# A bidirectional mLSTM in chunks of 128 tokens with a carried state, and three experts asked for in routing, in a two-layer float32 kernel

## What is computed

```python
b = jnp.cumsum(lf, axis=-1)
d_log = jnp.where(tril, b[..., :, None] - b[..., None, :] + ig[..., None, :], -jnp.inf)
inter = b + m_st[..., None]
m_t = jnp.maximum(inter, jnp.max(d_log, axis=-1))
s = jnp.einsum('bhtd,bhsd->bhts', q, k) * jnp.exp(d_log - m_t[..., None])
w_inter = jnp.exp(inter - m_t)
num = einsum(s, v) + w_inter[..., None] * einsum(c_st, q)
den = jnp.sum(s, axis=-1) + w_inter * einsum(n_st, q)
h = num / jnp.maximum(jnp.abs(den), jnp.exp(-m_t))[..., None]
c_new = decay * c_st + einsum(ws, v, k);  n_new = decay * n_st + einsum(ws, k)
...
h_m = rmsnorm(h_fwd + h_bwd, g_mlstm) * sigmoid(o)
```

## Time and profile before

| | |
|---|---|
| median of the timed runs | 3332.91 us (3331.67, 3332.91, 3337.18) |
| the profiled execution | 3332.51 us |
| its span, first to last instruction | 3330.8 us |
| PE busy, of the span | 2955.4 us (89%) |
| DVE, ACT, POOL busy | 1328.8, 585.3, 345.6 us (40%, 18%, 10%) |
| granted TensorE clock, mean | 0.949 |
| moved by DMA | 356.83 MB, mean 107 GB/s |

### The profile page before, as it was taken

How to read it: one execution, slowest core, us unless ns; L and a number is a source line. 1 busy time by engine, 2 the same in 40 slices (tenths; PEclk the granted TensorE clock), 3 DMA queues, 4 the chain that set the end, 5 groups by cost and what they waited for, 6 DMA issues and landing times. The chain is left out here.

```text
span 3330.8 us, 42568 instructions
## 1 busy us (share of the span) xinstructions
PE 2955.4 (89%) x17472; PEld 2247.0 (67%) x17472; DVE 1328.8 (40%) x2355; ACT 585.3 (18%) x1386; POOL 345.6 (10%) x511
## 2 busy tenths in 40 slices
PE   5988788999999999999999899888996949888883
PEld 4855566567777788888888788677875845455551
DVE  4645555822224442434343564453525351111114
ACT  2213213810000210100000241332002011111111
POOL 1011131000000100000000100452002011111112
PEclk9989899999999999999999999898998969999997
DMA  3100012011112111111112431001110259999995
GB/s 123 51 13 1 1 38 82 30 53 38 50 48 98 37 47 57 38 51 51 51 41 62 90 50 27 2 2 37 51 32 9 109 211 381 416 413 408 405 369 214
DMA packets 127058, 356.83 MB, mean 107 GB/s; under 512 B 14089, under 2 KB 58377, under 8 KB 109457
## 3 DMA queue, kind: packets, MB, share of 16 engines
q1 hardware_dynamic: 114464, 336.09, 28.0%
q0 software_dynamic: 10512, 16.80, 1.3%
q10 hardware_dynamic: 1888, 1.22, 0.1%
HBM read 343.18 MB, written 31.46 MB: 112 GB/s over the span
## 5 line engine op out<-in xcount | busy, mean ns | idle before, releaser
L427 PE MATMUL banks<-hT_upper,split_weights 128*128 128x512 f32 x2304 | 746.4, 401 | 15.1 <-PEq L193 8.6
L427 PEld LDWEIGHTS banks<-hT_upper,split_weights 128*128 128x128 f32 x2304 | 435.9, 189 | 117.0 <-issue 22.1
L418 PE MATMUL banks<-split_weights,hT_upper 128*128 128x512 f32 x1536 | 485.4, 398 | 22.5 <-DVE hT_lower L136 9.0
L427 PE MATMUL banks<-hT_lower,split_weights 128*128 128x512 f32 x1152 | 451.4, 392 | 0.0
L418 PEld LDWEIGHTS banks<-split_weights,hT_upper 128*128 128x128 f32 x1536 | 292.4, 192 | 85.8 <-issue 18.7
L418 PE MATMUL banks<-split_weights,uT_upper 128*128 128x512 f32 x1024 | 315.9, 390 | 0.0
L418 PE MATMUL banks<-split_weights,hT_lower 128*128 128x512 f32 x768 | 304.5, 396 | 0.0
L2784 PE MATMUL banks<-expert,ex_xT 128*64 128x256 f32 (+1 forms) x1632 | 263.5, 399 | 45.7 <-DMA expert<-in_w_up 21.2
L427 PEld LDWEIGHTS banks<-hT_lower,split_weights 128*128 128x128 f32 x1152 | 218.2, 189 | 54.9 <-issue 11.2
L2784 PEld LDWEIGHTS banks<-expert,ex_xT 128*64 128x64 f32 (+1 forms) x1632 | 171.4, 150 | 101.4 <-issue 60.1
L418 PEld LDWEIGHTS banks<-split_weights,uT_upper 128*128 128x128 f32 x1024 | 192.1, 188 | 39.5
(11 more groups left out here) (452 smaller groups left out, 3810.7 us busy)
## 6 DMA issues: line engine op xcount, KB each, us to landing
expert<-in_w_gate SPq DMA_DIRECT2D x51, 1024.0 KB, 13.3
expert<-in_w_up SPq DMA_DIRECT2D x51, 1024.0 KB, 22.2
expert<-in_w_down SPq DMA_DIRECT2D x51, 1024.0 KB, 24.9
raw_weights<-in_w_in SPq DMA_DIRECT2D x38, 1024.0 KB, 5.5
raw_weights<-in_w_up SPq DMA_DIRECT2D x16, 1024.0 KB, 5.3
raw_weights<-in_w_down SPq DMA_DIRECT2D x16, 1024.0 KB, 5.0
hT<-in_w_gate SPq DMA_DIRECT2D x13, 1024.0 KB, 11.6
hT<-in_w_up SPq DMA_DIRECT2D x13, 1024.0 KB, 23.4
```

Source lines behind the costliest of these rows:

```text
L418: last = pe.matmul(bank, acts[x][:, r * KT // 2 + k, m * P:(m + 1) * P].bitcast(F32R), w[y][:, k, :].bitcast(F32R), start=(r == 0 and k == ...
L427: last = pe.matmul(out, w[x][:, k, c0:c0 + P].bitcast(F32R), acts[y][:, k, t0:t0 + nt].bitcast(F32R), start=(k == 0 and x == y), stop=(k = ...
```

## The change

`mlstm_inputs` gets two more rows and a small one: with `m_end` the maximum at a chunk's last token (in the direction's order) and `m_ref` that of the chunk before, `W` = m_ref - M (the state's weight at each token), `WS` = A - m_end (a key's weight in the state), and `dec_row` = m_ref - m_end (the state's own decay, 8x8). `T1`, `W`, `WS` and `dec_row` are exponentiated by ACT at i == 15.

`mlstm` is written anew. Its 16 units (N = 2 x TT) are one chunk of 128 tokens in one direction, for all four heads; directions alternate, forwards from chunk 0 and backwards from chunk 7 (`unit`). Units 0 to 7 (n < DONE) meet a chunk for the first time, units 8 to 15 for the second, when the sum over both directions can be normalized and gated. A unit's weights are one 128x512 tile; banks: 0 for the maxima, 1 for the decays, 2 and 3 for the scores, 4 to 7 in two pairs for numerators, denominators and state updates. The weights, weighted keys and maxima of unit n + 2 and the scores of n + 1 are asked for ahead of unit n's products. The old `Pt` of [P, (TT * (TT + 1) + KT) * P] becomes `work` of [P, KT * S + 2 * S].

In the diff, `x` in engine rows is the memory that holds queries and keys, `ml_work` is `work`.

```diff
-def mlstm_inputs(c, hT, whole, qk_raw, qkT, v_sb, og, row):
+def mlstm_inputs(c, hT, whole, qk_raw, qkT, v_sb, og, row, dec_row):
...
-                    nc.scalar.activation(row(T1), row(T1), ACT.Exp)
+                    for r in (T1, W, WS):
+                        nc.scalar.activation(row(r), row(r), ACT.Exp)
+                    nc.scalar.activation(dec_row, dec_row, ACT.Exp)
...
+            s_dve.done(nc.vector.tensor_tensor(by_chunk(W), along(m_ref), by_chunk(M), ALU.subtract))
+            s_dve.done(nc.vector.tensor_tensor(by_chunk(WS), by_chunk(A), along(m_end), ALU.subtract))
+            s_dve.settle(dve)
+            nc.vector.tensor_tensor(dec_row, m_ref[:, :], m_end[:, :], ALU.subtract).then_inc(m_ready, 1)
...
+            def m_rows(n):
+                d, j = unit(n)
+                if n:
+                    pe.wait_ge(exp_done, n)
+                for h in range(M_HEADS):
+                    last = nc.tensor.matmul(c.bank(0)[:, h * P:(h + 1) * P], c.k["pick8"][:, 4 * d + h, :], row(M)[:, chunk(j)],
+                                            start=True, stop=True)
+                last.then_inc(mrow_there, 1)
...
+            def scores(n):
+                d, j = unit(n)
+                if n:
+                    pe.wait_ge(weighted, n)
+                for i in range(2):
+                    for h, b, rows_of in heads_of(i):
+                        last = nc.tensor.matmul(SCORES[:, b, i * P:(i + 1) * P], qkT[rows_of, 2 + i, chunk(j)],
+                                                qkT[rows_of, i, chunk(j)], start=True, stop=True)
+                last.then_inc(scores_there, 1)
...
+            for n in range(N):
+                d, j = unit(n)
+                if n + 2 < N:
+                    m_rows(n + 2)
+                if 2 <= n + 1 < N:
+                    decays(n + 1)
+                if n + 1 < N:
+                    scores(n + 1)
...
+                elif n < DONE + 2:
+                    pe.wait_ge(first_taken, n - 1)
+                else:
+                    pe.wait_ge(second_taken, n - 1 - DONE)
+                if n < N - 2:
+                    pe.wait_ge(kw_ready, n + 1)
+                    for i in range(2):
+                        for h, b, half_rows in heads_of(i):
+                            nc.tensor.matmul(c.psum[half_rows, out_bank(n) + i, 2 * V1:3 * V1], k_weighted[:, n % 4, h, :],
+                                             v_sb[:, j, h, :], start=True, stop=True)
...
+                pe.wait_ge(weighted, n + 1)
+                for i in range(2):
+                    for h, b, rows_of in heads_of(i):
+                        if n >= 2:
+                            nc.tensor.matmul(c.bank(out_bank(n) + b)[:, i * V1:(i + 1) * V1], q_scaled[rows_of, n % 2, i, :],
+                                             state[rows_of, d, i, :], start=True, stop=False)
+                    for h, b, _ in heads_of(i):
+                        last = nc.tensor.matmul(c.bank(out_bank(n) + b)[:, i * V1:(i + 1) * V1], weights[:, n % 4, place(h), :],
+                                                v_sb[:, j, h, :], start=(n < 2), stop=True)
+                last.then_inc(out_there, 1)
...
+        @block.scalar
+            for n in range(N):
...
+                if n + 2 < N:
+                    exps(n + 2)
+                if n < DONE:
+                    act.wait_ge(r_ready, n + 1)
+                    for h in range(M_HEADS):
+                        last = nc.scalar.activation(h_of(t, h), num(n, h), ACT.Copy, scale=r_den[:, n % 2, place(h):place(h) + 1])
+                    last.then_inc(first_taken, 1)
+                else:
+                    act.wait_ge(second_taken, n - DONE + 1)
+                    for h in range(M_HEADS):
+                        s_act.settle(act)
+                        last = nc.scalar.activation(junk[:, :], h_of(t, h), ACT.Square, accum_out=ss[:, t, h:h + 1])
...
+        @block.vector
+            for n in range(N):
+                if n + 1 < N:
+                    weigh(n + 1)
+                    if n + 1 >= 2:
+                        scale_q(n + 1)
+                if n < N - 2:
+                    update(n)
+                finish(n)
+                if n - 1 >= DONE:
+                    gate(n - 1)
...
+EARLY = 3
...
-            for i in range(SLOTS - 1):
+            for i in range(EARLY):
                 expert = experts.number(sp, slice(i, i + 1))
...
-            gate_up(SLOTS - 1)
-            down(SLOTS - 1)
+            sp.wait_ge(idx_ready, 2)
+            for i in range(EARLY, SLOTS):
+                gate_up(i)
+                down(i)
```

More of the change, by code:

```diff
@@ L1 @@
+import math
 from contextlib import ExitStack
@@ L624, in copy_out, with unit, chunk @@
[L624 to L627, removed]
-        block = mem.enter_context(nc.Block())
+        block = mem.enter_context(nc.Block())
+        I, X, T1, DCUM, A, M, W, WS = range(8)
+        def unit(n):
+            return n % 2, n // 2 if n % 2 == 0 else TT - 1 - n // 2
+        def chunk(j):
+            return slice(j * P, (j + 1) * P)
@@ new lines, in heads_of, with out_bank, num, h_of @@
+        def heads_of(i):
+            return [(2 * i + b, b, slice(b * M_QK, (b + 1) * M_QK)) for b in range(2)]
+        def out_bank(n):
+            return 4 + 2 * (n % 2)
+        def num(n, h):
+            return c.bank(out_bank(n) + h % 2)[:, h // 2 * V1:h // 2 * V1 + M_V]
+        def h_of(t, h):
+            return hs[:, t // 2, t % 2, h * M_V:(h + 1) * M_V]
+        def place(h):
+            return 2 * (h % 2) + h // 2
+        SCORES = c.psum[:, 2:4, 0:HALF]
+        K_PAIRS = [(j, TT - 1 - j) for j in range(TT // 2)]
@@ new lines, in _ @@
+            for which, r in ((0, A), (1, T1), (2, WS)):
+                for m in range(TT):
+                    nc.tensor.transpose(c.bank(4)[:, which * 64 + m * 8:which * 64 + m * 8 + 8], row(r)[:, chunk(m)], c.k["ident"][0:8, 0:8])
+            for d in range(2):
+                for i in range(2):
+                    for h, b, half_rows in heads_of(i):
+                        last = nc.tensor.matmul(c.psum[half_rows, 5, (2 * d + i) * TT:(2 * d + i + 1) * TT], c.k["pick8"][:, 4 * d + h, 0:M_QK],
+                                                dec_row, start=True, stop=True)
@@ new lines, in update @@
+            def update(n):
+                d, j = unit(n)
+                dve.wait_ge(out_there, n + 1)
+                for i in range(2):
+                    new = c.bank(out_bank(n) + i)[:, 2 * V1:3 * V1]
+                    old = state[:, d, i, :]
+                    if n < 2:
+                        last = nc.vector.tensor_copy(old, new)
+                    else:
+                        last = nc.vector.scalar_tensor_tensor(old, old, dec[:, d, i, j:j + 1], new, ALU.mult, ALU.add)
+                    if i == 0:
+                        s_dve.done(last)
+                s_dve.settle(dve)
+                last.then_inc(state_ready, 1)
@@ new lines, in gate @@
+            def gate(m):
+                t = unit(m)[1]
+                dve.wait_ge(rstd_ready, m - DONE + 1)
+                for h in range(M_HEADS):
+                    last = nc.vector.scalar_tensor_tensor(h_of(t, h), h_of(t, h), rstd[:, t, h:h + 1], og[:, t, h * M_V:(h + 1) * M_V],
+                                                          ALU.mult, ALU.mult)
+                last.then_inc(gated, 1)
+            copy_k(0)
+            weigh(0)
+            for p in range(1, 4):
+                copy_k(p)
@@ new lines, in _ @@
+            for n in range(N):
+                if n + 1 < N:
[7 more added lines that the diff above has]
+                    gate(n - 1)
+            gate(N - 1)
+            for m in range(DONE + 1, N, 2):
+                dve.wait_ge(hT_there, m - DONE + 1)
+                nc.vector.tensor_copy(qkT[:, :, chunk(unit(m)[1])], c.bank(m - DONE).rearrange("p (a n) -> p a n", a=4))
```

354 lines of the change are left out of this document (181 added, 173 removed).

## The result

| | before | after |
|---|---|---|
| median of the timed runs | 3332.29 us (3330.45 to 3337.18, 4 runs) | 3250.97 us (3245.43 to 3263.79, 4 runs) |
| profiled execution, its span | 3332.51, 3330.8 us | 3255.43, 3253.6 us |
| mLSTM block | 207.4 us | 138.7 us |
| expert stage, SP's first issue to the end | 618.6 us | 616.8 us |

After over before is 0.9759, 95% interval 0.9726 to 0.9792: **81 us faster**, where 102 were forecast (3230.5 us). The changed kernel's times spread over 18 us, those of the kernel before over 7.

A forecast was written before the change was run, and what follows sets the result against it. It took the mLSTM block as bound by engines' work and handovers, the expert stage by DMA bytes. Block 207.4 to 109 us (98.5) plus experts 3.5 gave 102 off 3332.5: 3230.5 us, range 3213 to 3274.

The forecast's parts named there:

- ahead of the loop, with the cold start: mLSTM block's start: transposes, decay factors, first row maxima, table load and exponentials, 11 us, plus 4 for cold start.
- 16 units, handovers, clock drops: mLSTM loop: 16 units less what first and last leave out, 77.4 us, plus 3 for handovers and 4 for drops.
- expert edit, gain: Expert stage: three experts asked for early instead of four, first gather lands 5 us earlier; net gain 3.5 us.
- 8 us for the clock: mLSTM block: allowance for half clock, 4 us for the cold start and 4 for drops as in the delta rule.
- Rival 1: mLSTM block stays at half clock, every unit PE-bound at 9.2 us, block 163 us, kernel 3285 us; chance 0.20.
- mixture: mLSTM block between full clock and the half clock of rival 1, kernel around 3255 us; chance 0.07.
- the case that the forecast stood on: mLSTM block at full clock, kernel 3215 to 3246 us; chance 0.58.
- rival 2: mLSTM unit costs what a retention chunk does, 6.9 us bound by its own chain; block 129, kernel 3251 us; chance 0.11.
- ACT's chain: mLSTM second half: row maxima wait for ACT's exponentials, which stand behind its squares; 5.4 us a unit.
- the 3 us for handovers: mLSTM block: handovers not counted elsewhere, as PE's last product must land, a few tenths a unit; 3 us.
- the prediction's own estimate of a drain: mLSTM units: 0.27 us per change of tile form instead of 0.15, 1 us more a unit, 16 us in all.
- Rival 3: mLSTM block: no overlap between units, 12.75 us each, block 224 us, kernel 13 us slower at 3346 us; chance 0.01.

The follow-up runs named there:

- full_rows: The change, with the products of row maxima and decays reading 128 rows, 120 of them zeros, instead of 8: 3216.7 us, ratio 0.9652.
- hot_start: full_rows with 13 more dense products, read by nobody, on PE at the end of mlstm_inputs: 3213.6 us, ratio 0.9649.
- warm: full_rows for units 0 to 5, with 8-row products of row maxima and decays from unit 6 on: 3251.0 us, ratio 0.9749.
- maxima_full: The change, with 128 rows only in the products of the row maxima, the decays left at 8: 3214.3 us, ratio 0.9653.
- the two fillers: The change with two more unread 256-column products per unit from the third on: of 128 rows 3230.6 us, of 8 rows 3285.4 us.

## Why the prediction was right in kind and wrong in size

| term | forecast | measured, the change | measured, full_rows |
|---|---|---|---|
| ahead of the loop, with the cold start | 15 | 13.3 | 12.7 |
| 16 units, handovers, clock drops | 84.4 | 116.7 | 73.3 |
| behind the last products | 9 | 8.7 | 8.7 |
| mLSTM block, sum | 108.4 | 138.7 | 94.7 |
| expert edit, gain | 3.5 | 4.1 (means of stages) | |

Without its 8 us for the clock the forecast is 100.4, which full_rows' 94.7 answer to. The loop is counted from the row maxima of unit 2, at 220.1 us, to the end of the last values' products, at 336.8 (220.2 and 293.5 in full_rows), so that 43 of the 44 us between the two blocks lie in it:

```profile
336.07 0.71 PE L773 MATMUL banks<-v_m,ml_work 128*128 128x129 f32 x4
```

**The term that failed is the clock.** The prediction took "4 us for the cold start and 4 for drops as in the delta rule (0.96 over some 80 us)". Measured, the change's block is 44 us longer than the one of full_rows, which differs from it by rows of zeros and, for a few us, by one change of tile form a unit; and 2.4 of full_rows' 94.7 are cold start (hot_start). The step that went wrong is the choice of the row: of the earlier trace rows the window at 251 to 254, PE busy throughout and 0.50 granted right behind 4 us of nothing but 8-row products, was the nearest to this block, and the delta rule, with 0.96, has no such products in it. I set against it that "scores to values are 3.4 us of dense work in each unit", and took it for granted that work by which PE is busy is work that holds the clock. It did not: 0.50 at 18.00 of 18.00 us busy.

**Rival 1 is what happened,** for most of the block. It said 9.2 us a unit where 9.04 were measured, from a price of 4.9 where a unit with eight changes of form takes 5.03 at full clock, and a ratio of 1.87 where 9.04 / 5.03 is 1.80: two small errors that nearly cancel. The block had a mean clock of 0.60 and not 0.50, since there were full-clock stretches near 230 and 245, and for the most part from 322 us on. So the time fell where the prediction had its mixture, "around 3255", with a chance of 0.07. That was too little: clock states that change within the block were a case of their own, next to "always up" and "always down", and they are what the prediction's own windows of other stages (0.96) show. The time lies inside the stated range of 3213 to 3274, but not by the case that the forecast stood on (full clock, 3215 to 3246). It is also the 3251 of rival 2, by luck: units there cost 6.9 us with PE idle, and here 9.04 with PE busy.

**At full clock the working holds.** PE's unit was priced at 4.9 us and is 5.03 with the eight changes of form that were priced (warm) and 4.85 with seven (full_rows): 0.99, 0.59, 0.64 and 0.59 for maxima, decays, scores and update, and 2.04 for the two rounds. For the second half 5.4 us a unit were worked out from ACT's chain. In full_rows the row maxima of unit 12 begin at 266.61 and those of unit 14 at 276.98, two units apart, 5.2 us each, and in front of both PE waits for ACT as the prediction said. These are the only two such waits: the earlier units of the second half still take 4.85.

```profile
266.61 1.16 PE L707 MATMUL banks<-ml_m_row,c_pick_wide 128*128 128x128 f32 x8 [0.41 <-ACT ml_work L814]
271.56 1.06 PE L707 MATMUL banks<-ml_m_row,c_pick_wide 128*128 128x128 f32 x8
276.98 1.16 PE L707 MATMUL banks<-ml_m_row,c_pick_wide 128*128 128x128 f32 x8 [0.40 <-ACT ml_work L814]
```

In the change itself this loop is hidden, since 9.04 is more than 5.2. In full_rows the loop of 73.3 us has no room for the 3 us for handovers: PE is busy for 18.00 of 18 us in the first half, and the forecast's 5.4 for all eight units of the second was too much.

**The change of tile form** was put at 0.15 us, and the prediction's own estimate of a drain, 0.27, would have added 16 us. (The Trainium skill, TensorEngine Tiling (Array Packing), "Key Properties", says that a change of tiling mode drains TensorE, and gives no time for it.) At 288.01 in full_rows the state products follow the scores in the same form, without a change between them. Elsewhere there is one on either side: the scores take 0.64 us to the next row (233.69 to 234.33) and the state products 0.43 (234.92 to 235.35). Here it is 0.55 and 0.32:

```profile
287.46 0.71 PE L728 MATMUL banks<-x 64*128 64x128 f32 x8
288.01 0.39 PE L791 MATMUL banks<-ml_work 64*128 64x129 f32 x4
288.33 0.71 PE L794 MATMUL banks<-v_m,ml_work 128*128 128x129 f32 x4
```

So a change costs about 0.09 us in the row ahead of it and 0.10 in the row behind, 0.19 together, and the 0.18 between 5.03 and 4.85 says the same. The trace agrees with the skill that a change has a price; its size lies nearer to the 0.15 of the sum than to 0.27. Eight of them are 1.5 us of a unit.

**Small terms.** The masking of 128x512 was taken at 1.05 us and took 0.64, a plain value between the bounds of 0.29 and 1.2; nothing hung on it. The row work in mlstm_inputs was costed at nothing, with DVE's 4.03 us of idle time as its cover, and cost 0.16. Rival 2 (6.9 us a unit from retention's own chain) is out: with the clock up, PE never idles in the first half. Rival 3 is out by the overlap that the trace shows.

**Experts.** The mechanism was right: the first use 5 us earlier was 4.5, and a short hole took the place of the first and of most of the second. The rule weighed against it (the Trainium skill, DMA: Bandwidth & Descriptors, "Queues, rings and completion order": queues share an engine packet by packet) was taken to give 0. The trace disagrees with that conclusion for this gather, 9.4 us behind four experts and 4.7 or 5.3 behind three, though the gathers of the stage still land after 9.0 in the median; whether the turns themselves are as the skill has them, no run here shows.

## What to carry to other kernels

Price a stretch of small products twice, at 1.00 and at 0.50, and decide between them by a row of the same rows and columns, not by how busy PE is. Where PE is the bound and its clock low, try to pad the contraction to 128 rows with zeros. It costs no product and no column, but memory and the time to write the zeros (here on an idle engine): in this kernel it gave another 34 us, two fifths of what the whole change gave. Of the versions here full_rows, maxima_full and hot_start are the fastest, 3214 to 3217 us, 0.965 of the kernel before; between them the measurement can't choose.

## What the runs showed of the hardware

- PE can be busy without a gap and stay at half clock for 54 us (260 to 314 us). The Trainium skill (TensorE: Matmul & The Clock Gate, "Part 1: The HAM clock gate") has the clock follow how busy PE has recently been. By that rule this stretch would run at 2.4 GHz. The trace disagrees, and the two fillers show what matters: with the added products at the same places, the clock from 260 to 278 us is 1.00 with 128 rows in them and 0.50 with 8.
- Rows of zeros count as rows at work, in this kernel. In full_rows 120 of the 128 rows that carry the maxima are zeros in both operands, and the clock is 1.00.
- Work that does nothing can shorten a kernel: 28 dense products that nobody reads made it 20 us faster.
- A change of tile form costs PE about 0.19 us at full clock, half of it in the row ahead and half behind (full_rows at 288.01; 5.03 against 4.85 us a unit).
- The stretch from the block's end to the experts takes one of two lengths, 2290 to 2292 or 2295 to 2298 us, in kernels whose code there is the same. Two profiled executions can differ by 6 us on that alone.
